# Moving a batch's weighting and attention's value product in the order of four engines

## What is computed

```python
# softmax attention: two maps per head, one value product
p = softmax(s1, axis=-1) - lam * softmax(s2, axis=-1)
o_b = einsum('bhqk,bkhv->bqhv', p, v)
# channel part: 8 heads x 16 experts for each token t
act = gelu(einsum('td,thkd->thk', x, peer_u[idx]))
y = einsum('thk,thkd->td', g * act, peer_v[idx])
```

## Time and profile before

| | us |
|---|---|
| median of 3 runs | 4809.88 |
| lowest and highest run | 4796.96 and 4827.41 |
| the profiled execution's own time | 4809.88 |
| its span, first to last instruction | 4808.1 |
| PE busy with matmuls (65%) | 3137.2 |
| DVE busy (56%) | 2689.4 |
| ACT busy (27%) | 1308.3 |
| POOL busy (26%) | 1246.6 |

### The profile page before, as it was taken

How to read it: one execution, slowest core, us unless ns; L and a number is a source line. 1 busy time by engine, 2 the same in 40 slices (tenths; PEclk the granted TensorE clock), 3 DMA queues, 4 the chain that set the end, 5 groups by cost and what they waited for, 6 DMA issues and landing times.

```text
span 4808.1 us, 46328 instructions
## 1 busy us (share of the span) xinstructions
PE 3137.2 (65%) x14944; PEld 1915.3 (40%) x14944; DVE 2689.4 (56%) x7493; ACT 1308.3 (27%) x2814; POOL 1246.6 (26%) x1067
## 2 busy tenths in 40 slices
PE   6887846886797268865974397885559843333333
PEld 4675734553465035633743164552237520000000
DVE  2133145678535766786345755576542466675675
ACT  2344102455301034565010225544330200000000
POOL 0000002323223232333222322222121224444453
PEclk8886978887898578987987597787779865555555
DMA  7322439997899799988998887776577969999998
GB/s 265 131 77 90 170 103 366 365 359 298 339 362 409 281 395 361 372 314 325 366 365 328 315 322 260 275 275 250 195 265 286 350 244 371 411 408 389 395 407 338
DMA packets 284681, 1466.27 MB, mean 305 GB/s; under 512 B 46344, under 2 KB 103528, under 8 KB 118392
## 3 DMA queue, kind: packets, MB, share of 16 engines
q0 software_dynamic: 152064, 1107.36, 58.9%
q1 hardware_dynamic: 132376, 355.94, 20.7%
HBM read 1426.39 MB, written 35.68 MB: 304 GB/s over the span
## 4 chain that ended last, share of the span: by engine, by line
PE 43%; DMA 29%; DVE 13%; issue 6%; ACT 6%; SPq 2%; POOL 0%; DVEq 0%; ACTq 0%; POOLq 0%
DMA rt_ring<-in_peer_uv,rt_few_idx 15%; PE pair L567 10%; PE pair L556 9%; PE rt_acc L807 7%; PE bank L567 5%; PE bank L556 4%; DVE rt_ring L1580 4%; DMA w<-out_v_prompt 3%; PE pair L722 2%; PE bank L736 2%; DMA w<-in_weights 2%; DMA out_v_prompt<-dense 2%; DMA w<-out_v_sample 2%; DMA scratch_scores<-dense 2%; DVE rt_diag L1591 1%
## 5 line engine op out<-in xcount | busy, mean ns | idle before, releaser
L1633 POOL DMA_INDIRECT rt_ring<-in_peer_uv,rt_few_idx x1056 | 1243.3, 1177 | 3533.0 <-PE rt_acc L807 2602.7
L1580 DVE SCALAR_TENSOR_TENSOR rt_ring<-rt_ring,rt_h 128x1024 f32<-128x1024 f32 x1056 | 1264.2, 1220 | 456.6 <-DMA rt_ring<-in_peer_uv,rt_few_idx 435.8
L807 PE MATMUL rt_acc<-rt_ring,rt_diag 128*32 128x512 f32 x4224 | 811.9, 846 | 999.7 <-DVE rt_diag L1591 999.3
L807 PEld LDWEIGHTS rt_acc<-rt_ring,rt_diag 128*32 128x32 f32 x4224 | 102.0, 126 | 1445.1 <-DVE rt_diag L1591 1291.9
L567 PE MATMUL pair<-dense,w 128*128 128x256 f32 (+1 forms) x2336 | 552.7, 395 | 18.3 <-DMA w<-in_weights 17.4
L556 PE MATMUL pair<-w,dense 128*128 128x256 f32 (+1 forms) x2288 | 545.0, 396 | 17.5 <-DMA w<-in_weights 12.8
L1142 ACT ACTIVATE rt_act_dot<-rt_dot 128x2 f32<-128x2 f32 x528 | 106.3, 202 | 1578.4 <-DVE rt_ring L1580 1576.8
L567 PEld LDWEIGHTS pair<-dense,w 128*128 128x128 f32 x2336 | 446.4, 194 | 143.2 <-issue 48.2
L556 PEld LDWEIGHTS pair<-w,dense 128*128 128x128 f32 (+1 forms) x2288 | 427.5, 190 | 159.3 <-issue 63.6
L1591 DVE TENSOR_SCALAR rt_diag<-cst,rt_act_dot,rt_few_prob 128x32 f32<-128x32 f32 x1056 | 265.9, 297 | 185.8 <-ACT rt_act_dot L1142 169.5
L722 PE MATMUL pair<-w,dense 64*128 64x512 f32 (+3 forms) x448 | 137.8, 741 | 254.2 <-DMA w<-out_v_prompt 117.8
(11 more groups left out here) (236 smaller groups left out, 3066.8 us busy)
## 6 DMA issues: line engine op xcount, KB each, us to landing
w<-in_weights SPq DMA_DIRECT2D x232, 1024.0 KB, 7.1
rt_ring<-in_peer_uv,rt_few_idx POOLq DMA_INDIRECT x1056, 10.9
rt_h<-scratch_h SPq DMA_DIRECT2D x132, 128.0 KB
dense<-scratch_mod SPq DMA_DIRECT2D x18, 512.0 KB, 11.2
dense<-in_x_prompt SPq DMA_DIRECT2D x16, 512.0 KB, 9.3
scratch_scores<-dense SPq DMA_DIRECT2D x64, 128.0 KB, 7.2
rt_sc<-scratch_scores SPq DMA_DIRECT2D x8, 1024.0 KB, 9.4
rt_x<-scratch_x SPq DMA_DIRECT2D x132, 32.0 KB
```

The costliest lines, as they stand in the source:

```text
L807: mm = nc.tensor.matmul(acc[u % 2][a * T:(a + 1) * T, :], diag[b % 2][:, i, :], slot[:, D + c * BANK:D + (c + 1) * BANK], start=(q == 0), ...
L1580: dt = nc.vector.scalar_tensor_tensor(up, up, 1.0, h2[u % 2][:], ALU.mult, ALU.mult, accum_out=dot[:, b % 2, i:i + 1])
L1633: nc.gpsimd.indirect_dma_start(ring[n % RING][:], None, d["peer_uv"], bass.IndirectOffsetOnAxis(ap=few_idx[u % 2][:, c:c + 1], axis=0)).th ...
```

## The change

Two things are moved; no operation is added or taken away.

`order`: on DVE the list of a step becomes `dots` of b, the lane, `weigh` of b. So `weigh` is done in the step of its own batch, behind the lane. On ACT, `dots` of b stands behind the whole lane. PE's list is the same. (SP's and POOL's list now names `dots` too, for which they have nothing to do.)

`attend` on PE: the block for `apply` stands at the head of the row, before `out`, `turn` and `score`. Its waits are the same.

```diff
@@ -278,22 +278,20 @@
 def order(engine):
 
     fill, steps = sequence()
-    items, last = list(fill), NU * NB - 1
+    items = list(fill)
     for b, ticked, units in steps:
-        lane, half, cut, spent = [i for i, _ in ticked], sum(c for _, c in ticked) / 2, 0, 0.0
-        while cut < len(ticked) and spent < half:
-            spent += ticked[cut][1]
-            cut += 1
-        before = [("weigh", b - 1)] if b else []
+        lane = [i for i, _ in ticked]
         if engine == "tensor":
-            items += lane[:cut] + before + lane[cut:]
+            half, cut, spent = sum(c for _, c in ticked) / 2, 0, 0.0
+            while cut < len(ticked) and spent < half:
+                spent += ticked[cut][1]
+                cut += 1
+            items += lane[:cut] + ([("weigh", b - 1)] if b else []) + lane[cut:]
         elif engine == "scalar":
-            items += lane[:cut] + [("dots", b)] + lane[cut:]
-        elif engine == "vector":
-            items += [("dots", b)] + before + lane
+            items += lane + [("dots", b)]
         else:
-            items += lane + [("weigh", b)] + units
-    return items + ([("weigh", last)] if engine in ("tensor", "vector") else [])
+            items += [("dots", b)] + lane + [("weigh", b)] + units
+    return items + ([("weigh", NU * NB - 1)] if engine == "tensor" else [])
@@ -686,6 +684,20 @@
                 if k == 0:
                     for b in range(6):
                         pe.wait_ge(bank_free[b], counts[b])
+                if row["apply"] is not None:
+                    x, first, last, G = row["apply"]
+                    h, ti = units[x]
+                    t = GROUPS[g][ti]
+                    n, tiles = width(t), key_tiles(t)
+                    v = W[WPOS[g, "kv" if t < NT else "kvs", h] % NW][:, D:].rearrange("p (t c) -> p t c", c=VD)
+                    pe.wait_ge(at_copied, session_of[G] + 1)
+                    if first == 0:
+                        pe.wait_ge(at_rescaled, base + x)
+                    for kt, w in tiles[first:first + 4]:
+                        mm = nc.tensor.matmul(bank[5][0:n, 0:VD], mixT[0:w, G % 2, (kt - first) * P:(kt - first) * P + n], v[0:w, kt, :],
+                                              start=(kt == 0), stop=(kt == len(tiles) - 1))
+                    mm.then_inc(at_applied, 1)
+                    released[g, "kv" if t < NT else "kvs", h] = (at_applied, G + 1)
                 for h, s in row["out"]:
```

More of the change, by code:

```diff
@@ L725, in attend @@
                                 mm.then_inc(at_scored[m], 1)
[L726 to L738, removed]
-                    released[g, "kv" if t < NT else "kvs", h] = (at_applied, G + 1)
             def merge(g, i):
```

## The result

The changed kernel takes 4955.59 us (median of 4 runs, 4949.23 to 4960.73), the kernel before 4815.14 us on the same chip. The ratio is 1.0294, with a 95% interval from 1.0257 to 1.0332: 2.9% slower, 140 us by the medians. The forecast was +80 us, 4890. In the profiled execution the span is 4958.9 us, 150.8 more than before, and PE's mean granted clock is 0.737 (0.754 before).

The account below looks back on a forecast made before the run. Full DMA engines bound plain matrix lanes, a chain across engines softmax attention. Terms 50+16+9+20+0-15 = +80 us on 4809.88 us gave 4890 us, own range 4850 to 4935, 8-in-10 range 4780 to 5010.

Parts of the forecast that it names:

- the prediction's own sign: Forecast wrong if first gather to last stage's start doesn't grow 50 to 100 us, or PE hardly awaits the rescale.
- Linear attention, +50: In 21 linear-attention steps, the next batch's dot products on DVE delay the following piece by 2.36 us each: +50 us.
- Fill, +16: First group, no batches: rescale and apply join PE's chain, 2.0 us a head, 8 heads: +16 us.
- Second group, +9: Second group's attention: longer chain through rescale and apply, six heads 110.6 us instead of 100.1, less 1.5: +9 us.
- Third group, +20: Third group's attention: chain of 13.2 us a unit, +1.3 for each of 16 units: +20 us.
- Fourth group, 0: Fourth group's attention: earlier key and value loads gain 20 us, first two heads lose about as much: 0.
- Earlier slots, -15: Ring slots come free one batch's dot products earlier, removing part of DVE's waits for gathers: -15 us.
- every step pays: Rival: lanes of any kind end in ACT work, so DVE waits for gelu before dot products; 5047 us, chance 0.12.
- The clock: Rival: matmuls in the chain of 48 score rows run at PE's lower clock, 58 us on top, 4950 us; chance 0.05.

## Why the prediction was right and where it was short

The direction and the mechanism held: DVE waits for G, PE waits for the rescale, the last stage is untouched. The size was short: 4955.59 us against a forecast of 4890 and an own range up to 4935; only the wide range held it. By the prediction's own sign, 50 to 100 us more from the first gather to the last stage, the size was wrong: by batch times that stretch grew by 135. By the steps of the sum:

**Linear attention, +50.** Right in size, as the run on it alone shows (+54), and the place above shows the mechanism as told. But D behind W with G left in place costs 24 us in these stretches by the table (DVE's list alone); the rest needs G's new place too, which the term left out.

**Fill, +16.** Nearly right. PE's applies in the first group of the changed kernel:

```profile
397.36 1.19 PE L697 MATMUL bank<-w,dense 128*128 128x128 f32 x4 [1.36 <-DVE dense L1393]
...
406.75 1.19 PE L697 MATMUL bank<-w,dense 128*128 128x128 f32 x4 [1.36 <-DVE dense L1393]
```

A head takes 9.39 us, not the 10 of the prediction (8.02 before): 8 x 1.37 = 11 us, 13 by the first gather.

**Second group, +9.** The sum is right for six heads and its parts are not. Scores and apply of the changed kernel in full swing, PE and then DVE:

```profile
1135.17 1.65 PE L734 MATMUL pair<-w,dense 64*128 64x384 f32 x4 [0.99 <-ACT dense L937]
...
1199.80 1.62 PE L697 MATMUL bank<-w,dense 128*128 128x128 f32 x6 [5.09 <-DVE dense L1393]
...
1202.20 1.52 PE L734 MATMUL pair<-w,dense 64*128 64x384 f32 x4
...
1208.99 2.05 PE L697 MATMUL bank<-w,dense 128*128 128x128 f32 x8 [4.28 <-DVE dense L1393]
...
1212.84 2.08 PE L734 MATMUL pair<-w,dense 64*128 64x512 f32 x4
...
1223.66 1.65 PE L734 MATMUL pair<-w,dense 64*128 64x384 f32 x4
...
1244.84 1.65 PE L734 MATMUL pair<-w,dense 64*128 64x384 f32 x4
```

```profile
1205.80 0.51 DVE L1589 TENSOR_SCALAR rt_diag<-cst,rt_act_dot,rt_few_prob 128x32 f32<-128x32 f32 x2 [0.58 <-ACT rt_act_dot L1140]
1206.21 1.22 DVE L1578 SCALAR_TENSOR_TENSOR rt_ring<-rt_ring,rt_h 128x1024 f32<-128x1024 f32 x1
...
1208.50 0.34 DVE L1393 TENSOR_SCALAR dense<-bank,recip 128x128 f32<-128x128 f32 x1
```

The chain is the predicted one: scores, maxima, W, D, rescale, apply, transposes, scores. But from the fourth head on a head takes 1223.66 - 1202.20 = 21.46 us where I had 16.3 without loads and 19.5 with them. Here each row holds a whole W and D and not 0.8 of one, and W waits for G (0.58 us here). Loads no longer show at all. The first two heads take less than I had, about 7 and 12 us, and by chance six heads make 1244.84 - 1135.17 = 109.7 us (110.6 predicted).

What I left out comes behind the last scores. There the lane is `merge`, whose ACT work waits for PE, and G is now behind it. DVE's waits for G in this stretch, of the changed kernel (1277 to 1379 us) and, in the second fence, of the kernel before (1236 to 1320 us):

```profile
DVE rt_diag L1589 <- ACT rt_act_dot L1140: 25.1, 8, 7.2
```

```profile
DVE rt_diag L1591 <- ACT rt_act_dot L1142: 2.4, 1, 2.4
```

The windows of the same stretch, from the last scores to the gathers of batch 78, of the changed kernel and of the kernel before:

```profile
1277.00:1379.00 102.00, 74.64 (x351) 50.02 (x351) 43.39 (x109) 26.57 (x54) 25.33 (x22) 0.77 0.82 301
```

```profile
1237.00:1320.00 83.00, 70.75 (x354) 49.22 (x354) 43.08 (x108) 28.13 (x55) 23.29 (x22) 0.90 1.00 393
```

The same work takes 102 us and not 83. Before, the DMA engines were full there; now they are not, so the new waits turned a DMA-bound stretch into a chain. G's place is not the whole of it: the stretch takes 92 us with apply alone, 93 with the order alone, 90 with DVE's list alone and 85 with ACT's list alone. So half of the 19 us comes with apply at the head, whose last rows run here, and most of the order's half with W in its own step.

**Third group, +20.** The first and last scores of the changed kernel:

```profile
2155.26 2.50 PE L734 MATMUL pair<-w,dense 64*128 64x512 f32 x8 [0.99 <-ACT dense L937]
...
2359.72 2.93 PE L734 MATMUL pair<-w,dense 64*128 64x512 f32 x8 [1.84 <-ACT dense L1079]
```

The chain was sized about right: 15 units take 2359.72 - 2155.26 = 204.5 us, 13.6 each (13.2 predicted), against 178.4 before: +26. It is apply's part: from batch 172 to 210 apply alone loses 31 us and the order alone 3. Half as much again, 13 us, is lost ahead of it in the keys, by G behind copies that wait for stores, which the prediction doesn't have.

**Fourth group, 0.** Wrong by 12 us: from the first scores to the last it takes 3694.47 - 3348.03 = 346.4 us, and 3548.41 - 3214.12 = 334.3 before:

```profile
3214.12 2.20 PE L722 MATMUL pair<-w,dense 64*128 64x512 f32 x8
...
3548.41 2.03 PE L722 MATMUL pair<-w,dense 64*32 64x512 f32 x8 [12.50 <-DMA w<-out_v_sample]
```

The tile does come back earlier, by more than I said; the changed kernel's first and last scores, and waits for loads between them:

```profile
3348.03 2.96 PE L734 MATMUL pair<-w,dense 64*128 64x512 f32 x8
...
3506.60 2.02 PE L734 MATMUL pair<-w,dense 64*32 64x512 f32 x8 [5.40 <-DMA w<-out_v_sample]
...
3554.71 2.02 PE L734 MATMUL pair<-w,dense 64*32 64x512 f32 x8 [5.31 <-DMA w<-out_v_sample]
...
3694.47 2.02 PE L734 MATMUL pair<-w,dense 64*32 64x512 f32 x8 [5.50 <-DMA w<-out_v_sample]
```

5.4 us in place of 12.56. But a head takes 48.1 us, longer than the 46.7 of before: what the load gave was taken again, as I read it by the chain through rescale, W and D. Alone, apply makes this stretch 5 us shorter and the order 2 us longer, so the 12 us come from both together; no run takes them apart further. With apply at the head alone and only from the third head on, where the order is the old one, a head takes 43.0.

**Earlier slots, -15.** No gain shows in the whole. Gathers are waited for 90 us less (345.5 against 435.8), but the wait for G has grown by 366. With DVE's list alone the wait for gathers falls just as far (344.9), and that profiled execution loses 24 us in linear attention and ends level with the kernel before, so something is won back elsewhere. No run isolates the term.

**The missing term.** It is G's place. I priced ACT's list only where the last work of the lane came from DVE. Yet the same edit puts G behind every copy and every exponential that waits for something else, for a store or for PE, and W, now ahead of everything that follows on DVE, hands that wait on. Shown is +13 us at the third group's keys, where ACT's list alone loses 12, and the part of the +50 that DVE's list alone doesn't make. In the 19 us behind the second group's attention and the fourth group's 12 it has a share at most. The rival *every step pays* had a wait for G in any kind of lane right, and too high a price, since it took D's 2.36 us for 100 steps; the loss lies in fewer places, the largest waits being near 15 us.

*The clock* is lower too: eight matmuls of M take 1.06 us or 1.94 in the changed kernel, and the stretch behind the second group's attention has gone from a granted 0.90 to 0.77 with the new waits. Its share was not measured apart. The rival's count is off: there are 56 rows of scores with batches beside them (16, 16 and 24), not 48.

## What to carry over

In a kernel whose engines each run their list in order, an instruction that waits for another engine belongs behind work that doesn't hang on that wait; moving it to "its own" step takes its cover away. Look on both sides of such a handover: what stands ahead of the producer on its engine matters as much as what stands behind the consumer, and copies that wait for a store or for PE are the dear ones. When an instruction is moved to the front because its result frees something early, move its own input forward too (here the rescale), or the wait for the load only changes its name; and choose the place by stage: by batch times, apply at the head with an early rescale won 14 us in the second group's attention and lost 11 in the third's.

## What was not expected

A cheap instruction can carry a long wait across three engines: a store of keys held ACT's copy for 8.20 us, G behind it, W behind G, and left DVE idle for 15.25 us.

The two halves of `order` are not additive (20 and 36 us alone, 85 together), while `order` and apply are so within the intervals (59 and 85 against 142), though both act on the chain of attention. And G as early as it can be, which all but ends DVE's wait for it, costs as much as apply at the head (+63 us), since ACT is the engine that then stands still.
